# A transformer layer with a PEER mixer on one core: where ScalarE takes the last two key-score blocks

## What is computed

```python
q = (xt @ w_query).reshape(tp, PEER_HEADS, 2, PEER_DKEY // 2)           # 8 heads
s = jnp.einsum('thpc,hpnc->thpn', q, sub_keys)                          # 16 blocks of 128 scores
sv, si = lax.top_k(s, PEER_TOPK)                                        # 16 of 128, twice per head
cand = sv[:, :, 0, :, None] + sv[:, :, 1, None, :]
best, pos = lax.top_k(cand.reshape(tp, PEER_HEADS, 256), PEER_TOPK)     # 16 of 256
ids = ...                                                               # which of 16384 experts
gates = jax.nn.softmax(best, axis=-1)
h = jax.nn.gelu(jnp.einsum('td,thkd->thk', xb, u_table[ids]))
out = jnp.einsum('thk,thkd->td', gates * h, v_table[ids])
```

## Time and profile before

| | us |
|---|---|
| median of 3 runs | 3962.62 |
| the runs | 3962.62, 3985.08, 3955.46 |
| the profiled execution, its own time | 3960.71 |
| its span, first to last instruction | 3958.9 |

### The profile page before, as it was taken

How to read it: one execution, slowest core, us unless ns; L and a number is a source line. 1 busy time by engine, 2 the same in 40 slices (tenths; PEclk the granted TensorE clock), 3 DMA queues, 4 the chain that set the end, 5 groups by cost and what they waited for, 6 DMA issues and landing times.

```text
span 3958.9 us, 64674 instructions
## 1 busy us (share of the span) xinstructions
PE 3792.9 (96%) x26604; PEld 3735.3 (94%) x26604; DVE 2230.4 (56%) x2933; ACT 939.1 (24%) x809; POOL 1820.6 (46%) x895
## 2 busy tenths in 40 slices
PE   8999998796999999999999999999999999999995
PEld 7999998796999999999999999999999999999995
DVE  4876967756899422111121112113688878877877
ACT  2333322313222222222222222222222222221223
POOL 3332332334333487788788885002344444443311
PEclk9999998898999999999999999999999999999998
DMA  3221221452235677777777777665578777777752
GB/s 139 84 74 61 84 80 62 165 228 103 85 107 165 208 199 198 194 202 201 193 193 201 201 200 194 198 201 199 224 286 320 286 294 308 289 294 294 288 208 87
DMA packets 449651, 751.76 MB, mean 190 GB/s; under 512 B 81344, under 2 KB 378752, under 8 KB 386320
## 3 DMA queue, kind: packets, MB, share of 16 engines
q1 hardware_dynamic: 321216, 543.27, 40.6%
q0 software_dynamic: 83968, 134.55, 11.8%
q10 hardware_dynamic: 44368, 72.67, 5.0%
HBM read 677.60 MB, written 207.00 MB: 223 GB/s over the span
## 4 chain that ended last, share of the span: by engine, by line
PE 82%; DVE 13%; DMA 1%; ACT 1%; issue 1%; POOL 1%; SPq 0%; DVEq 0%; ACTq 0%; POOLq 0%
PE ps L554 52%; PE ps L771 27%; DVE yb L1271 2%; DMA wraw<-in_v_t 1%; PE ps L680 1%; PE ps L630 1%; DVE dist L1159 1%; DVE qe L1190 1%; PE ps L676 1%; POOL wl L471 0%; PE ps L660 0%; DVE sif L1383 0%; ACT wh L828 0%; DVE si L1369 0%; DVE oh L1397 0%
## 5 line engine op out<-in xcount | busy, mean ns | idle before, releaser
L554 PE MATMUL ps<-xh,wh 128*128 128x272 f32 x5888 | 1234.4, 291 | 49.5 <-POOL xl L490 23.2
L554 PE MATMUL ps<-xh,wl 128*128 128x272 f32 x5888 | 1226.6, 290 | 0.0
L554 PE MATMUL ps<-xl,wh 128*128 128x272 f32 x5888 | 1222.8, 289 | 0.0
L554 PEld LDWEIGHTS ps<-xh,wh 128*128 128x128 f32 x5888 | 933.1, 190 | 62.2 <-issue 50.0
L513 POOL DMA_INDIRECT g_scratch<-picks,g_col x512 | 868.3, 1696 | 208.3 <-issue 182.6
L554 PEld LDWEIGHTS ps<-xl,wh 128*128 128x128 f32 x5888 | 934.2, 190 | 0.0
L554 PEld LDWEIGHTS ps<-xh,wl 128*128 128x128 f32 x5888 | 927.4, 190 | 0.0
L828 ACT ACTIVATE wh<-wraw 128x2048 fp32r<-128x2048 f32 x328 | 628.5, 1916 | 1125.3 <-PE ps L771 833.8
L1441 DVE TENSOR_TENSOR wl<-wraw,wh 128x2048 fp32r<-128x2048 f32 x114 | 261.5, 2294 | 1099.8 <-ACT wh L828 1099.8
L471 POOL TENSOR_TENSOR wl<-wraw,wh 128x2048 fp32r<-128x2048 f32 x88 | 430.9, 4899 | 804.8 <-ACT wh L828 804.8
L771 PE MATMUL ps<-Wh,wh 128*128 128x416 f32 x2048 | 720.8, 352 | 11.7 <-DVE Wl L1498 7.0
(11 more groups left out here) (234 smaller groups left out, 2515.5 us busy)
## 6 DMA issues: line engine op xcount, KB each, us to landing
wraw<-in_u_t SPq DMA_DIRECT2D x128, 1024.0 KB
v_rows<-in_v_t SPq DMA_DIRECT2D x256, 512.0 KB
wraw<-in_v_t SPq DMA_DIRECT2D x128, 1024.0 KB
wraw<-in_w_in SPq DMA_DIRECT2D x40, 1024.0 KB
g_scratch<-zeros ACTq DMA_DIRECT2D x32, 832.0 KB, 4.9
h_scratch<-hb ACTq DMA_DIRECT2D x64, 416.0 KB
gt<-g_scratch SPq DMA_DIRECT2D x16, 1664.0 KB, 10.7
hg<-h_scratch SPq DMA_DIRECT2D x16, 1664.0 KB, 15.6
```

Of the source, the lines that this page charges most:

```text
L554: ins = mat(out[:, h], w[:, u, k], m[:, k, halves[h]], start=(begin and k == ks[0] and w is wh and m is ah), stop=(end and k == ks[-1] and ...
```

## The change

ScalarE's order at the end of the queries is another. Before: the last query eviction, block 14, block 15, then the tiles of U. Now: the last query eviction, U's tile 0 (Gelu and the `wh` of tile 2), block 14, U's tile 1 (Gelu and the `wh` of tile 3), block 15, the first two stores, then U's tile 2. For this the loop over groups of four query tiles runs two times in place of three, and the last group is written out behind it without its last `score_evict`. No other engine's list changes.

```diff
-            with a.Fori(1, NQ // SC) as i:
+            with a.Fori(1, NQ // SC - 1) as i:
                 for j in range(SC):
                     q_evict(j % 2, i * SC + j, True)
                     score_evict(i * SC + (j - 1), (j - 1) % SC)
-            score_evict(NQ - 1, SC - 1)
+            for n in range(NQ - SC, NQ):
+                q_evict(n % 2, n, True)
+                if n < NQ - 1:
+                    score_evict(n - 1, (n - 1) % SC)
...
             def u_four(g, i, first=False):
                 for w in range(4):
                     u_tile(g * EG + (4 * i + w), w, first)
+                    if first and w < 2:
+                        score_evict(NQ - 2 + w, (NQ - 2 + w) % SC)
                     if w % 2:
                         h_store(g, 2 * i + w // 2)
```

## The result

The changed kernel took **3973.43 us** (median of 20 runs, 3945.19 to 3981.11), the kernel before 3958.96 us in the same comparison (20 runs, 3952.71 to 3985.08): 1.003 times as long, interval 1.0018 to 1.0041. The forecast was 3949 us with a range of 3941 to 3965. So the change lost some 14 us where it was to win 12. All runs of the changed kernel but one lie from 3967.73 to 3981.11; the one is 3945.19. The profiled execution took 3972.55 us (span 3970.7). Two runs in the comparisons further down (5358.68 us at a mean granted clock of 0.647, 4179.17 at 0.835) stand in the medians given with them and in nothing else.

The account below looks back on a forecast made before the run. TensorE, busy 96% of the span, was taken as the bound. Removing its 9.59 us stop and 2.26 us of low clock, 11.85 us, from 3960.71 gave 3948.9, taken as 3949 us; range 3941 to 3965.

Parts of the forecast that it names:

- The change, part by part: ScalarE's new order before U: written-out steps cost 0, tile 2's `wl` ends 4.7 us before TensorE wants it.
- The rule weighed: VectorE casts or two-input operations and GpSimd SBUF reads lock each other out: 4.3 us on VectorE at U's start, hidden.
- The sum: At U's second tile, TensorE's stop of 9.59 us and low clock of 2.26 us go: 11.85 us gained.
- so the whole of what comes after moves up: From U's tile 2 through V's stage, everything was to come 11.85 us earlier, V's waits staying 11.7 us.
- the scatter on GpSimd: Could stay where it was, but its last issue at 2444.9 is almost 290 us ahead of V's stage.
- Rival 1: V's stage: low clock's 2.26 us stay and 4.7 us of `wl` waits double; gain 4.9, 3956 us; chance 0.10.
- Rival 2: U's start: tile 2's `wl` still comes after 1206.2, as with late bytes; stop stays, 3960.7 us; chance 0.05.
- rival 3: At the Exp behind tile 11, ScalarE waits for a late VectorE; 50 us of delay gives 3972 us; chance 0.03.

Follow-up runs that it names:

- e1_pad: The changed kernel with 96 matmuls of no use added ahead of U's first tile, on chip 7: 3966.52 us, ratio 1.0028 to the kernel before.
- f1_after: The changed kernel once more, nothing altered, as control on chip 8: 3976.80 us, ratio 1.0038 to the kernel before.

## Why the prediction was wrong

**The change, part by part: right.** Every step of the TensorE chain came within 0.5 us: Gelu of tile 0 forecast at 1194.2, measured 1193.83; `wl` of tile 2 at 1196.9, 1196.56; block 14 at 1200.0 after a wait of some 3 us, 1199.58 after 3.17; Gelu of tile 1 at 1206.2, 1205.86; block 15 at 1208.8, 1208.33; `wl` of tile 3 at 1209, 1208.51. The table load does lie in ScalarE's idle time (1181.39). The written-out steps cost nothing (3960.84 against 3959.65). No wait of TensorE is left from 1160 us to V's stage.

**The rule weighed: as taken.** The addition behind the second CAST, `cand`, took 5.77 us from 1208.72, started 0.2 us behind a `wl` (1208.51 to 1213.14), so it ends 1.4 us behind it. That is the loss that I had put at 4.3 us on VectorE, and it was hidden: VectorE still waited 20.03 us for the Exp, within the forecast 12 to 21. This agrees with the section "Who interferes with whom" of the Trainium skill, page SBUF — State Buffer, that the prediction weighed.

**The sum: its term right, its last step wrong.** 11.85 us were forecast for stop and clock together; 12.2 were measured at tile 2 and at the last Gelu of U. 0.4 of these were there ahead of the change, at the last query eviction (1178.95 in place of 1179.34). From that eviction to the last Gelu of U it is 1554.0 to 1554.2 us in all five traces of the old order and 1542.3 in all fourteen of the new one (e1_pad's 96 matmuls aside): 11.7 to 12.0, the term as forecast. Where no run is held up, the whole comes out: ratios of 0.9965 and 0.9962 are gains of 13.9 and 15.0 us, with 11.85 inside both intervals (9.1 to 18.6 and 9.5 to 20.6); of the 2 to 3 us on top, 0.7 are TensorE's earlier full clock in V's first tile (below), and the rest is not accounted for (V's stage takes 1217.8 to 1223.0 us in the three undisturbed traces of the changed kernel, 1225.5 before). The medians of 3944.08 and 3943.82 lie inside the forecast range. The step that failed is "so the whole of what comes after moves up". I had read V's stage from one trace of before (11.7 us of waits) and carried it over unchanged, as if a stage had one duration. For what else could stay where it was I had looked at the scatter on GpSimd alone, and at none of the gathers behind it. V's stage took 1225.5 us before and 1249.5, 1254.0 and 1253.2 in the three held-up traces, 24 to 28.5 us more, and in three of the five rows of the table this befalls the new order in 32 of 36 runs, the old one, by its times, in 9 of 62.

**The range.** Its upper end came from rivals 1 and 2 and a little of rival 3, which is little more than "no gain". One of the three runs shown of the kernel before, 3985.08, lay 22.5 us above their median. I used it for a chance of 0.03, as mere spread, and asked for no mechanism. With the trace read for what could be so long, GpSimd's gathers at the start of V's stage were to be seen, though not what they would do.

**The rivals.** Rival 1 had the right place (V's stage) and the wrong price: 4.7 us of waits for `wl`, which measured 4.2. Rival 2 and rival 3 didn't occur: tile 2's bytes were there, and VectorE was 20 us early for the Exp. The true mechanism was in none of them.

**What stays open.** Shown: the hold-up occurs on some chips only (on chips 2 and 11 none of the new order's 24 runs with the gathers in place had it); on those, gathers at the very start of V's stage are needed and the load of group 1 is not; neither the written-out group nor absolute time explains it. Not settled: why the new order meets it in nine runs of ten and the old in one or two of ten. Counted from the last Gelu of U, the instructions of all engines stand at the same places, to some 0.1 us, until V's first tile is half done. Then one thing differs between the orders. VectorE's first two additions of V, one row (L1471, L1476 and L1482 in the kernels before, changed and e1_pad):

```profile
2751.75 1.21 DVE L1471 TENSOR_TENSOR acc<-acc,ps 128x416 f32<-128x416 f32 x2 [3.96 <-PE ps L771]
```
```profile
2738.78 1.25 DVE L1476 TENSOR_TENSOR acc<-acc,ps 128x416 f32<-128x416 f32 x2 [3.22 <-PE ps L771]
```
```profile
2748.21 1.21 DVE L1482 TENSOR_TENSOR acc<-acc,ps 128x416 f32<-128x416 f32 x2 [3.95 <-PE ps L777]
```

These are 18.3, 17.6 and 18.3 us behind the last Gelu (2733.42, 2721.21, 2729.91). TensorE starts V's products at a granted clock of 0.50. In stretches of 1 us counted from that Gelu it is 0.54 from 10 to 11 us and 1.00 from 11 on in the changed kernel, but 0.50 until 12 us and 0.72 (e1_pad: 0.73) from 12 to 13 in the other two. So the new order has TensorE 0.7 us further on against the gathers. The odds on the chips with a hold-up go the same way for the new order (32 of 36, against 9 of 62 in the old) but not cleanly: e1_pad, with the old order's timing, was held up in 5 of 10. It is a correlation that no run here tests. What is short during the hold-up, and why TensorE's signals are late ahead of it, isn't known either. That the old order's rare long runs are the same hold-up is likely by their distance (19 to 26 us above the median on chip 8), but none of them was profiled.

## What to carry to other kernels

A gain upstream is worth what the stage downstream makes of its new start: before a stage is carried over unchanged, look at the spread of the runs, and where one run of three lies 20 us off, ask which stage can take so much longer and price it in the range. Time a small gain on more than one chip, and put the changed kernel itself into every comparison as control; without it, two experiments here would have "shown" causes that were only another chip. A long row of small indirect gathers that nobody needs soon is best kept away from the first tiles of a dense TensorE stage: a wait of one tile cost nothing and removed the loss.

## What the runs showed of the hardware

- Beside a row of 38 indirect DMAs on GpSimd, 1.25 us apart, TensorE on some chips drops from one matmul per 0.19 us to mostly one per 1.4 to 3.5 us, in steps of 0.70 us, for some 30 us. TensorE's signals to VectorE and ScalarE were late before that, by 4.3 and then by 20 us, for matmuls that ran on time (the result's trace; waits of 19.97 and 27.27 us, "remote"), while GpSimd kept its pace. The DMA queues were nearly idle in part of it, so there bandwidth isn't what was short (f1_after, columns as in the stretches above):

```profile
2750.00:2766.00 16.00, 7.18 (x18) 3.52 (x16) 0.00 (x0) 0.00 (x0) 12.04 (x14) 0.67 0.02 0
2766.00:2782.00 16.00, 3.61 (x8) 2.29 (x9) 3.27 (x3) 1.91 (x1) 9.55 (x9) 0.50 0.66 245
2782.00:2786.00 4.00, 4.00 (x13) 3.82 (x12) 0.19 (x1) 0.00 (x0) 0.00 (x0) 0.50 0.17 68
```

- The clock follows: 0.67, then 0.50 (1.2 of 2.4 GHz), still 0.50 in the first 4 us in which TensorE is busy again, as behind the stop of before.
- The same program, in the same comparison with the same other kernel, is 0.4% slower on one chip and 0.4% faster on another.
